# A gate chunk moved to the end of the natural projection, and two small loads moved ahead of the cached keys, in a hybrid decoder step on one core

## The reference

```python
qa, ka, va, cq, ckv, kpe, ga, gb = jnp.split(h @ w_in, cuts, axis=-1)   # h = rms_norm(x), widths 512, 512, 512, 384, 256, 32, 1024, 1024
...
k_ext = jnp.concatenate([cache_win_k[i], ka], axis=1)                    # sample group: 1024 cached keys and 4 new ones
v_ext = jnp.concatenate([cache_win_v[i], va], axis=1)
o_a = combine_patterns([dilated_attn_sample(qa, k_ext, v_ext, w, d) for w, d in A_PATTERNS])
...
x = x + (jax.nn.sigmoid(ga) * ya + jax.nn.sigmoid(gb) * yb) @ w_o
```

## Time and profile before

| | us |
|---|---|
| median of 3 runs | 1953.53 |
| lowest and highest of them | 1952.35, 1954.16 |
| the profiled execution's own time | 1954.81 |
| span of the profiled execution (first to last instruction) | 1953.1 |
| PE busy in the span | 1879.2 |
| granted TensorE clock, mean over the span | 0.991 |

### The profile page before, as it was taken

One profiled execution on the slowest core, in us unless ns is written; L12 is line 12 of the kernel. 1 busy time (PEld: TensorE's weight loads), 2 busy tenths in 40 slices (PEclk: granted clock), 3 DMA queues, 4 the chain that ended last, 5 costly groups with the idle time before them and its releaser, 6 DMA issues.

```text
span 1953.1 us, 35100 instructions
## 1 busy us (share of the span) xinstructions
PE 1879.2 (96%) x13421; PEld 1739.2 (89%) x13421; DVE 795.7 (41%) x1748; ACT 501.6 (26%) x1058; POOL 767.6 (39%) x566
## 2 busy tenths in 40 slices
PE   8999989999899998899999999999999999999998
PEld 7977789999766666789999999999999999999997
DVE  5144112222846664785555421122112212255664
ACT  5232122233546553571122110010001000122222
POOL 5323122321514101104666663366346535666530
PEclk9999999999999999999999999999999999999999
DMA  7333275552012006405512321331133123311202
GB/s 235 106 122 129 93 218 168 176 177 69 12 32 62 6 1 203 126 3 169 185 54 86 130 86 54 128 128 46 54 130 129 46 73 130 107 44 43 87 22 89
DMA packets 185596, 193.40 MB, mean 99 GB/s; under 512 B 16506, under 2 KB 157658, under 8 KB 184834
## 3 DMA queue, kind: packets, MB, share of 16 engines
q1 hardware_dynamic: 168226, 161.85, 26.2%
q10 hardware_dynamic: 14816, 28.12, 4.1%
q0 software_dynamic: 2432, 1.74, 0.4%
HBM read 161.13 MB, written 63.97 MB: 115 GB/s over the span
## 4 chain that ended last, share of the span: by engine, by line
PE 50%; DVE 1%; POOL 1%; issue 1%; ACT 1%; DMA 0%; DVEq 0%; ACTq 0%; POOLq 0%
PE bank L657 16%; PE bank L658 16%; PE bank L659 16%; PE bank L2601 1%; POOL w_ple_lo L2289 0%; PE bank L2561 0%; DVE x_res L2496 0%; DMA f_gates<-gate_d 0%; POOL wu_lo_tail L2419 0%; DVE f_hg L2494 0%; ACT ple_sig L2360 0%; ACT tail_square L2367 0%; DVE f_tmp L2491 0%; PE bank L2526 0%; PE bank L2524 0%
## 5 line engine op out<-in xcount | busy, mean ns | idle before, releaser
L657 PE MATMUL bank<-h_hi,wu_hi_tail 128*128 128x352 f32 x960 | 310.3, 323 | 1.5 <-POOL wu_lo_tail L2419 1.5
L658 PE MATMUL bank<-h_lo,wu_hi_tail 128*128 128x352 f32 x960 | 307.8, 321 | 0.0
L659 PE MATMUL bank<-h_hi,wu_lo_tail 128*128 128x352 f32 x960 | 307.8, 321 | 0.0
L2417 POOL TENSOR_TENSOR wu_hi_tail<-w_stage_tail,ones 128x1024 fp32r<-128x1024 f32 x88 | 168.0, 1909 | 244.9 <-PE bank L659 161.8
L657 PE MATMUL bank<-a_hi,wu_hi_tail 128*128 128x352 f32 x768 | 247.7, 323 | 0.0
L658 PE MATMUL bank<-a_lo,wu_hi_tail 128*128 128x352 f32 x768 | 246.1, 320 | 0.0
L659 PE MATMUL bank<-a_hi,wu_lo_tail 128*128 128x352 f32 x768 | 245.9, 320 | 0.0
L2419 POOL TENSOR_TENSOR wu_lo_tail<-w_stage_tail,wu_hi_tail 128x1024 fp32r<-128x1024 f32 x88 | 219.3, 2492 | 6.9
L2370 ACT ACTIVATE a_hi<-f_hg 128x352 f32 x96 | 47.9, 499 | 597.8 <-DVE f_hg L2480 597.8
L2463 DVE TENSOR_TENSOR x_res<-bank,x_res 128x352 f32 x120 | 62.9, 524 | 301.7 <-PE bank L659 301.5
L657 PEld LDWEIGHTS bank<-h_hi,wu_hi_tail 128*128 128x128 f32 x960 | 180.1, 188 | 1.9 <-POOL wu_lo_tail L2419 1.8
(11 more groups left out here) (332 smaller groups left out, 3724.7 us busy)
## 6 DMA issues: line engine op xcount, KB each, us to landing
w_stage_tail<-in_w_up SPq DMA_DIRECT2D x32, 512.0 KB, 4.0
w_stage_tail<-in_w_down SPq DMA_DIRECT2D x32, 512.0 KB, 3.9
gate_d<-gate_out ACTq DMA_DIRECT2D x16, 528.0 KB, 3.3
f_gates<-gate_d ACTq DMA_DIRECT2D x24, 352.0 KB, 3.9
w_stage_gates<-in_w_in SPq DMA_DIRECT2D x16, 512.0 KB, 6.8
ws_ring<-in_cache_win_k SPq DMA_DIRECT2D x8, 1024.0 KB, 5.9
ws_ring<-in_cache_win_v SPq DMA_DIRECT2D x8, 1024.0 KB, 6.6
ls_keys<-in_cache_ckv SPq DMA_DIRECT2D x64, 128.0 KB, 2.5
```

The source lines that it names most:

```text
L657: pe.matmul(out, w, a, start=n == 0, stop=False)
L658: pe.matmul(out, w, b, start=False, stop=False)
L659: last = pe.matmul(out, v, a, start=False, stop=n == len(ks) - 1)
L2417: pool.tensor_tensor(g.wu_hi[:, j], g.w_stage[:, j], one, ALU.mult).then_inc(g.w_hi, 1)
```

## The change

Three edits, in two stages:

- PE's stream in the natural projection gets chunk 1 of the gates (unit 0, tokens 352 to 703, PSUM bank 1) behind its last product. It waits for the split of unit 0 and for ACT to have taken product 41 (t = 5 of block 4), the last one that used bank 1. It signals nothing. In the gates stage chunk 1 is left out of PE's row, and chunk 0 signals `full` twice, so that DVE and ACT go on as before.
- SP issues the loads of the new queries and keys (with the wait for the stores of `q_d`, `k_d` and `v_d` ahead of them) before the cached keys and values of sequence 0.
- PE transposes the new queries and keys behind chunk 2 and not behind chunk 1, and DVE copies them there.

```diff
--- before.py
+++ after.py
@@ -480,6 +480,10 @@
             for s in range(2 * NT, 5 * NT):
                 product(s)
 
+            pe.wait_ge(g.w_split, g.units + 1)
+            pe.wait_ge(n_got, 5 * NT - 3)
+            multiply_chunk(pe, g, 1, 0, 1, [(k, k) for k in range(KD)], g.h_hi, g.h_lo, signal=0)
+
         @block.scalar
         def _(act):
             def high_block(b):
@@ -795,11 +799,11 @@
                     sp.wait_ge(turned, TURNS * ((e - 3) // 2) + SK)
                 load_cached_window(sp, g.cache_win_v, s, ring[e % 3], ring_in[e % 3])
 
-            load_keys(0)
-            load_values(0)
             wait_stored(sp)
             sp.dma_start(q_new[:, :], g.q_d[SEQ:, :]).then_inc(new_in, 16)
             sp.dma_start(k_new[:, :], g.k_d[SEQ:, :]).then_inc(new_in, 16)
+            load_keys(0)
+            load_values(0)
             sp.wait_ge(clear, 1)
             for k in range(H // 2):
                 sp.dma_start(mask[NS * k:NS * k + 2 * TDEC, :], g.mask_ws_c[2 * TDEC * k:2 * TDEC * (k + 1), :]).then_inc(mask_in, 16)
@@ -901,8 +905,9 @@
                     pe.wait_ge(g.w_split, U + m + 1)
                 if n >= NCH:
                     pe.wait_ge(g.free, C + n - NCH + 1)
-                multiply_chunk(pe, g, c, m % 2, c, [(k, k) for k in range(KD)], g.h_hi, g.h_lo)
-                if n == 1:
+                if n != 1:
+                    multiply_chunk(pe, g, c, m % 2, c, [(k, k) for k in range(KD)], g.h_hi, g.h_lo, signal=2 if n == 0 else 1)
+                if n == 2:
                     turn_new()
                 for s, phase in samples_at(n):
                     turn_tiles(s, tiles_of[phase])
```

## The result

The changed kernel takes 1958.81 us, median of 17 runs (1954.26 to 1961.45); the kernel before takes 1954.53 in 17 runs (1949.39 to 1957.04), the three runs shown ahead of the prediction among them. The ratio is 1.0023, 95% interval 1.0016 to 1.0030: slower by 4.3 us, where 4.2 was forecast. Two further sets of 11 runs gave 1.0020 (1.0011 to 1.0029) and 1.0030 (1.0020 to 1.0039). The profiled execution took 1959.64, with a span of 1957.9.

The account below looks back on a forecast made before the run. Chunk 6 waits for unit 2's split weights, a chain hanging on SP's start; +1.6 (later start), +1.1 (extra store) and +1.5 (low clock) make +4.2 us, 1957.7 us against the median of 1953.53, range 1955.4 to 1959.9.

Parts of the forecast that it names:

- Part 1: Chunk 1 at the natural projection's end: PE becomes last at the barrier, SP starts the gates stage later, +1.6 us.
- (d): Rival: PE's extra chunk doesn't move the barrier, so no shift; +2.6 us, 1956.1; chance 0.06.
- Part 2: Two small loads first in SP's queue: new-key hole of 4.82 us closes, but unit 2's load keeps its position; 0.
- Part 3: PE's earliness puts one more ACT store ahead of unit 2's load; +1.1 us, bounds 0 and 1.6.
- Part 4: At chunk 6 PE's clock is down after a 13 us wait; +1.5 us, ends 0 and 3.1.
- (a): Rival: same chain but cheap, extra store hidden and clock back early; +2.1 to +3.3 us, 1955.6 to 1956.8; chance 0.22.
- (b): Rival: the clock stays down as at 575.6; +5.8 us, 1959.3; chance 0.12.
- (c): Rival: the new order relieves the DMA engines, unit 2's chain shortens; -4.4 us, 1949.1; chance 0.08.

Follow-up runs that it names:

- c: Changed kernel, plus SP issuing the loads of gate units 2 and 3 directly behind the cached keys of sequence 0; 1941.07 us, 0.9938 of before.
- b: Kernel before, with only the two small loads first and the transposes behind the third chunk, no chunk moved; 1.0012 of before, +2.3 us.
- a: Changed kernel with only the moved chunk kept, SP's order and the transposes' place as before; 1.0002 of before, +0.4 us.
- e: Changed kernel, with ACT's stores of gate units 0 and 1 held until unit 2's weights have landed; 1956.37 us, 1.0009 of before.
- i: e plus 64 unread matmuls on PE in the wait at chunk 6; 1.0005 of before, +1.0 us.
- d: Kernel before, plus only the loads of gate units 2 and 3 directly behind the cached keys of sequence 0; 1.0017 of before, +3.3 us.
- f: Changed kernel plus 80 unread matmuls on PE between chunks 5 and 6; 1.0002 of before, run again 1.0008.
- g: c without the moved chunk: small loads first, transposes behind the third chunk, units 2 and 3 early; 1945.34 us, 0.9949 of before.
- h: b plus 40 unread matmuls on PE between chunks 5 and 6; 1.0005 of before, +1.0 us.

## Why the prediction was right

**What bounds.** The reading that decided the forecast, that chunk 6 starts when unit 2 is split and that PE's gain up to there is spare time, is shown by c (the cause removed, 16.8 us inside the stage) and by b (the hole removed, chunk 6 not earlier by 0.1).

**Part 1**, +1.6: the seam grew by 1.52 in all kernels with the moved chunk. SP's first issue stands 4.18 us behind the end of the last natural matmul, where 4.2 was forecast. PE is last at the barrier; rival (d) is out.

**Part 2**, 0: SP's first issue stands 0.04 behind the block's start, new keys without a wait, PE at chunk 6 26.9 us behind the last natural matmul where 27.5 was forecast (270.5 less 243.04). The cover that I named, the moved chunk ahead of the wait for the stores, is real: without it b waits 0.65.

**Part 3**, +1.1 with 0 and 1.6 as bounds: the chain grew by 1.71, 1.19 and 0.83 us in three profiles, 1.24 in the mean. All three are taken against one profile of before; a, which has SP's order of before and no early store, has 34.79 where before has 35.50, so the base itself is known only to some 0.7 us. The mechanism is right, as e and i show, and so is the size: with both stores early the chain ends at 36.92 in the mean of five profiles, with both held at 34.72 in the mean of two. That is 2.2 us for two stores, an estimate of 1.1 for one if they share alike, where the bytes of one were priced at 1.6. By the Trainium skill (DMA: Bandwidth & Descriptors, section Queues, rings and completion order) each DMA engine goes round the queues that have work, so that the store takes its share at once; the trace agrees in so far as the store of 257.06 landed in 7.6 us while SP went on issuing loads. That the full 1.6 would be paid, as I had worked out from this rule, is not what the means show, though one profile, with 1.71, lies above it.

**Part 4**, +1.5: this term was mis-sized. Chunk 6 took 5.76, 6.71 and 6.12 us instead of 4.02, +2.18 in the mean, inside the bounds of 0 and 3.1. Two errors went into it. The stretches of the earlier trace rows are shorter than what they stand for: the low clock at the first hole lasted from 247.1 to 250.4, 3.4 us and not 2.70, and at 575.6 it was low for 6.3 us behind PE's return, not 5.60. And the two short ones were taken for the rule: they stand behind waits of 2.61 and 4.49 us. Behind the seven waits of 7.7 us and more in these profiles none was as short: from PE's return on the clock was low for 3.8, 5.9 and 4.6 us in the changed kernel, 5.8 in b, 4.8 in e, 7.0 in a and 6.9 in d.

**The sum** inside the stage is 1.52 + 1.24 + 2.18 = 4.94 against 4.2 (the stage itself: 4.93 in the mean of three). The time over 17 runs moved by 4.3 to 4.5; that it reads 1958.81 and not 1957.7 comes almost wholly from before, which has 1954.53 in 17 runs and had 1953.53 in three. That the last figure meets the forecast so closely is partly luck: single profiles have 1455.5 to 1461.9 us from the first matmul of the next stage to the end of the span, in kernels that are the same there, so the rest of the program scatters by more than the difference.

**Rivals.** (a), cheap, and (b), the clock down as at 575.6, were the two sides of the same terms; inside the stage the truth lies between the forecast and (b). (c) is excluded by the chain, which grew in all three profiles, and (d) by the seam.

## What to carry to other kernels

A wait of the bounding engine is worth its length only if the next thing that engine waits for is not already bound by something else: follow each later wait back to its own start before pricing the first. Here a wait of 1.27 us, third in size, decided that removing 7.4 us of larger ones would lose time, and moving two more loads forward in the same queue, those of the bounding weights, turned the loss into 12 us gained. An engine that arrives early also lets its results be stored early, beside the transfers that it will wait for, and can then stand idle long enough to lose its clock.

## What the runs showed of the hardware that I had not expected

The low clock behind a wait varies more than its cause. It lasted 3.8, 5.9 and 4.6 us behind waits of 14.85, 14.33 and 14.00 us in three profiles of one kernel at one place, and 7.0 us behind the shorter wait of 9.44 us in a. The added time of chunk 6, 1.74, 2.69 and 2.10 us, can thus be read from a single profile only to within about a microsecond.

Whether the clock falls at all isn't told by the length of a short wait. Waits of 1.69, 2.09 and 2.39 us behind dense work (f twice, i) and the 2.61 us at g's seam left it at 1.00; 2.17 us in h, and 2.60 or 2.61 us at the seam of before, b, d and h, did not. Nor does it have to fall during the wait: at before's seam it fell at 247.1, 1.0 us after PE was back, and in h 0.9 us after chunk 6 had begun.
